# Two stacked transformer blocks on one core: GpSimd's splits in four pieces, query scales moved into the copies out of PSUM, and another order at the start of each layer's projections

## The reference

```
x = layer_norm(alpha * x + 0.5 * swiglu(x, ffn_w_gu[l, 0], ffn_w_down[l, 0]), ln_g[l, 0], ln_b[l, 0])
mix = token_mixers(x, w_in[l], ...)
x = layer_norm(alpha * x + mix, ln_g[l, 1], ln_b[l, 1])
x = layer_norm(alpha * x + 0.5 * swiglu(x, ffn_w_gu[l, 1], ffn_w_down[l, 1]), ln_g[l, 2], ln_b[l, 2])
```

```
s = jnp.einsum('bqhgd,bkhd->bhgqk', qi, k).astype(jnp.float32) * scale
p = jax.nn.softmax(s, axis=-1)
o = jnp.einsum('bhgqk,bkhd->bqhgd', p.astype(v.dtype), v)
```

## Time and profile before

| | us |
|---|---|
| median of 3 runs | 1860.24 |
| lowest, highest | 1855.27, 1863.33 |
| profiled execution | 1861.57 |
| its span | 1859.8 |
| TensorE busy | 1660.4 (89%) |
| VectorE busy | 867.8 (47%) |
| ScalarE busy | 661.6 (36%) |
| GpSimd busy | 242.7 (13%) |
| mean granted TensorE clock | 0.939 |

### The profile page before, as it was taken

The page is one execution under the profiler, slowest core; times in us unless marked ns, Lnnn a source line. Parts: engine busy times, 40 slices in busy tenths (PEclk is TensorE's granted clock), DMA queues, the critical chain, the costliest instruction groups (busy, mean ns, idle before and its releaser), DMA issues.

```text
span 1859.8 us, 29654 instructions
## 1 busy us (share of the span) xinstructions
PE 1660.4 (89%) x11817; PEld 1325.8 (71%) x11817; DVE 867.8 (47%) x1292; ACT 661.6 (36%) x965; POOL 242.7 (13%) x182
## 2 busy tenths in 40 slices
PE   8989997677667776999999999999999999899997
PEld 6777874343223332899977779998999977779996
DVE  4684542011101111555565656555655575665555
ACT  5454441111101111343433544444334333544442
POOL 1223210000000000000133323001300133232000
PEclk9999998887788888999999999999999999899999
DMA  9514476999999999945533055436454542054511
GB/s 387 181 47 142 176 271 262 426 425 426 426 426 426 426 426 402 357 170 186 198 138 134 1 182 204 178 120 247 170 197 175 198 152 103 7 211 179 191 45 45
DMA packets 60951, 421.41 MB, mean 227 GB/s; under 512 B 7008, under 2 KB 16064, under 8 KB 17216
## 3 DMA queue, kind: packets, MB, share of 16 engines
q1 hardware_dynamic: 59136, 409.13, 56.1%
q10 hardware_dynamic: 1728, 11.03, 1.7%
HBM read 419.08 MB, written 1.05 MB: 226 GB/s over the span
## 4 chain that ended last, share of the span: by engine, by line
PE 62%; SPq 13%; DMA 8%; DVE 5%; issue 4%; ACT 3%; POOL 3%; DVEq 0%; ACTq 0%; POOLq 0%
PE bank L964 26%; SPq L1618 13%; PE bank L1005 12%; DMA ring<-in_we 7%; PE bank L1697 6%; PE bank L1739 6%; PE bank L1765 2%; DMA ring<-in_wf 1%; PE bank L1882 1%; PE bank L1900 1%; PE bank L983 1%; POOL small L534 1%; PE bank L604 1%; PE bank L1877 1%; PE bank L990 1%
## 5 line engine op out<-in xcount | busy, mean ns | idle before, releaser
L964 PE MATMUL bank<-xh,wlu 128*128 128x256 f32 x1344 | 379.9, 283 | 0.0
L964 PE MATMUL bank<-xh,whu 128*128 128x256 f32 x1344 | 379.8, 283 | 0.0
L964 PE MATMUL bank<-xl,whu 128*128 128x256 f32 x1344 | 379.8, 283 | 0.0
L964 PEld LDWEIGHTS bank<-xh,whu 128*128 128x128 f32 x1344 | 257.0, 191 | 3.3
L964 PEld LDWEIGHTS bank<-xl,whu 128*128 128x128 f32 x1344 | 257.0, 191 | 3.3
L964 PEld LDWEIGHTS bank<-xh,wlu 128*128 128x128 f32 x1344 | 257.2, 191 | 0.0
L873 DVE TENSOR_TENSOR wlu<-ring,whu 128x2048 fp32r<-128x2048 f32 x84 | 196.1, 2334 | 50.9 <-ACT whu L868 50.9
L873 DVE TENSOR_TENSOR wld<-ring,whd 128x1024 fp32r<-128x1024 f32 x88 | 108.2, 1229 | 189.2 <-ACT whd L868 189.2
L868 ACT ACTIVATE whu<-ring 128x2048 fp32r (+1 forms) x88 | 167.1, 1901 | 3.0 <-DMA ring<-in_wf 3.0
L868 ACT ACTIVATE whd<-ring 128x1024 fp32r (+1 forms) x88 | 93.2, 1060 | 207.1 <-PE bank L1005 203.7
L604 PE MATMUL bank<-ring,xg 128*32 128x256 f32 x1472 | 110.4, 436 | 48.7 <-DMA ring<-in_we 46.3
(11 more groups left out here) (319 smaller groups left out, 2808.3 us busy)
## 6 DMA issues: line engine op xcount, KB each, us to landing
ring<-in_we SPq DMA_DIRECT2D x144, 1024.0 KB, 26.9
ring<-in_wf SPq DMA_DIRECT2D x88, 1536.0 KB, 6.6
ring<-in_w SPq DMA_DIRECT2D x52, 1024.0 KB, 4.8
more<-in_we SPq DMA_DIRECT2D x48, 1024.0 KB, 25.7
ring<-in_w SPq DMA_DIRECT2D x32, 256.0 KB, 3.6
ln<-in_ln ACTq DMA_DIRECT2D x6, 1024.0 KB, 4.8
bias<-in_bias ACTq DMA_DIRECT2D x2, 2048.0 KB, 7.8
bias<-in_bias SPq DMA_DIRECT2D x1, 2048.0 KB, 19.7
```

The source lines that it names most:

```text
L964: ins = pe.matmul(bank[4 + p][:, m * S:(m + 1) * S], w[p][:, cols], v[:, k], start=(k == 0 and n == 0), stop=(k == KD - 1 and n == 2))
```

## The change

- Every split by GpSimd (and its one copy to a high part) is issued as four operations on 512 columns instead of one on 2048. The semaphore goes up after the fourth.
- At the start of a layer's projections GpSimd splits the second chunk too, right behind the first; ScalarE makes its high part without waiting for the end of the feed-forward; VectorE no longer splits it, and makes high part and rest of x pair by pair.
- `pe_part` runs the first chunk in two rounds: all products with the high part of x, for which it waits for that part alone, then those with the rest.
- Axial and latent units have scale 1. Their queries are multiplied by 64 ** -0.5 and 96 ** -0.5 in the copy out of PSUM, which becomes a tensor_scalar; the scale of the maximum goes.

```diff
@@ -382,12 +382,12 @@
             q, _ = head_rows(qkT2, 8 + at_q // 2, 64 * (at_q % 2), 64)
             _, k = head_rows(qkT2, 7, 64 * kv, 64)
             c = C0 + 384 + 64 * kv
-            units2.append(Unit([q], [k], [proj2[:, t, c:c + 64] for t in range(NT)], 64 ** -0.5,
+            units2.append(Unit([q], [k], [proj2[:, t, c:c + 64] for t in range(NT)], 1.0,
...
-            units2.append(Unit([q], [k], [vm[:, t, h, :] for t in range(NT)], BQ ** -0.5,
+            units2.append(Unit([q], [k], [vm[:, t, h, :] for t in range(NT)], 1.0,
...
@@ -483,12 +487,16 @@
-        def low(eng, run, c):
+        def low(eng, run, c, step=None):
 
             eng.wait_ge(dh_ok, run.high + (c + 1))
             n, s = run.width(c), run.slots[c]
-            eng.tensor_tensor(slot_r[s][:, 0:n], slot[s][:, 0:n], run.highs[c % 2][:, 0:n].bitcast(F32),
-                              ALU.subtract).then_inc(dlp_ok if c < 2 else dlv_ok, 1)
+            step = step or n
+            for c0 in range(0, n, step):
+                part = slice(c0, c0 + step)
+                ins = eng.tensor_tensor(slot_r[s][:, part], slot[s][:, part], run.highs[c % 2][:, part].bitcast(F32),
+                                        ALU.subtract)
+            ins.then_inc(dlp_ok if c < 2 else dlv_ok, 1)
...
@@ -873,6 +881,13 @@
+        def ffn_low_pieces(eng, t, p, done):
+
+            for c0 in range(0, 2 * D, 512):
+                ins = eng.tensor_tensor(wlu[p][:, c0:c0 + 512], ring[:, ring_tile(t) + c0:ring_tile(t) + c0 + 512],
+                                        whu[p][:, c0:c0 + 512].bitcast(F32), ALU.subtract)
+            ins.then_inc(done, 1)
...
@@ -1171,17 +1186,15 @@
-            if then is None:
+            if paired:
+                for q in range(4):
+                    top(q)
+                    rest(q)
+            else:
                 for q in range(4):
                     top(q)
                 for q in range(4):
                     rest(q)
-            else:
-                for q in range(4):
-                    top(q)
-                    rest(q)
-                    if q == 0:
-                        then()
...
@@ -1307,7 +1320,6 @@
                 run = run2(l, 0)
-                act.wait_ge(f_dn, (l * 2 + 1) * (FT + 1))
                 act_high(act, run, 1)
                 act_norm(act, st, l * 3)
...
@@ -1359,11 +1371,7 @@
-                def second():
-                    dve.wait_ge(dlp_ok, run.low_p + 1)
-                    low(dve, run, 1)
-
-                dve_norm_T(dve, l * 3, xTh2, (0, 1), second)
+                dve_norm_T(dve, l * 3, xTh2, True)
...
@@ -1419,9 +1427,10 @@
-                def group(n, b, inc=1):
+                def group(n, b, inc=1, scale=1.0):
                     dve.wait_ge(t_ps, tb + (n + 5 if n < 3 else n + 7))
-                    dve.tensor_copy(qkT2[:, 2 * n:2 * n + 2].rearrange("p k s -> p (k s)"), bank[b][:]).then_inc(t_out, inc)
+                    dve.tensor_scalar(qkT2[:, 2 * n:2 * n + 2].rearrange("p k s -> p (k s)"), bank[b][:], scale, None,
+                                      ALU.mult).then_inc(t_out, inc)
...
@@ -1453,13 +1462,14 @@
                     if u == 7:
-                        group(4, 6)
+                        group(4, 6, scale=64 ** -0.5)
                     if 9 <= u < 13:
                         j = u - 9
                         dve.wait_ge(t_ps, tb + (12 + j))
                         at_b = 10 + 4 * (j % 2) + 2 * (j // 2)
-                        dve.tensor_copy(qkT2[0:BQ, at_b:at_b + 2, :],
-                                        bank[7 - j % 2][0:BQ].rearrange("p (b s) -> p b s", b=2)).then_inc(t_out, 1)
+                        dve.tensor_scalar(qkT2[0:BQ, at_b:at_b + 2, :],
+                                          bank[7 - j % 2][0:BQ].rearrange("p (b s) -> p b s", b=2),
+                                          (BQ ** -0.5, 1.0)[j % 2], None, ALU.mult).then_inc(t_out, 1)
@@ -1513,7 +1523,8 @@
-                low(pool, run2(l, 0), 0)
+                for c in range(2):
+                    low(pool, run2(l, 0), c, 512)
                 for i in range(NT):
                     pool.wait_ge(var_ok, l * VAR2 + (VAR1 + 1 + i))
                     inverse_root(pool, rs[:, i:i + 1])
@@ -1552,9 +1563,11 @@
                 pool.sem_inc(hi_go, 1)
-                pool.tensor_copy(run.highs[0], slot[run.slots[0]]).then_inc(dh_ok, 1)
+                for c0 in range(0, CH, 512):
+                    ins = pool.tensor_copy(run.highs[0][:, c0:c0 + 512], slot[run.slots[0]][:, c0:c0 + 512])
+                ins.then_inc(dh_ok, 1)
                 for c in range(2):
-                    low(pool, run, c)
+                    low(pool, run, c, 512)
@@ -1679,7 +1692,10 @@
             for c in range(first, end):
-                if tb is not None:
+                split = tops is not None and c == first
+                if split:
+                    pe.wait_ge(xh_ok, tops)
+                elif tb is not None:
                     pe.wait_ge(t_out, tb + (c - first + 1))
...
@@ -1699,7 +1716,14 @@
-                if c < end - 1:
+                if split:
+                    for passes in ((0, 1), (2,)):
+                        if passes == (2,):
+                            pe.wait_ge(t_out, tb + 1)
+                        for kk in range(per):
+                            for i in range(NT):
+                                ins = products(kk, i, halves, passes)
+                elif c < end - 1:
...
@@ -1965,8 +1989,7 @@
             if unit.bias is None:
-                st.link(dve.tensor_reduce(nmax[:, b], src, X, ALU.max, negate=True))
-                dve.tensor_scalar(nmax[:, b], nmax[:, b], unit.scale, None, ALU.mult).then_inc(lg_ok, 1)
+                dve.tensor_reduce(nmax[:, b], src, X, ALU.max, negate=True).then_inc(lg_ok, 1)
                 return
...
@@ -2054,27 +2077,27 @@
-            low1(pool, 1)
+            low1(pool, 1, 512)
...
```

More of the change, by code:

```diff
@@ L458, in high1_of, with low1 @@
             act.activation(high1[n % 2], slot[n % SLOTS1], ACT.Copy).then_inc(dh_ok, 1)
-        def low1(eng, n):
+        def low1(eng, n, step=None):
             eng.wait_ge(dh_ok, n + 1)
-            eng.tensor_tensor(slot_r[n % SLOTS1], slot[n % SLOTS1], high1[n % 2].bitcast(F32),
-                              ALU.subtract).then_inc(low_at(n)[0], 1)
+            step = step or CH
+            for c0 in range(0, CH, step):
+                part = slice(c0, c0 + step)
+                ins = eng.tensor_tensor(slot_r[n % SLOTS1][:, part], slot[n % SLOTS1][:, part],
+                                        high1[n % 2][:, part].bitcast(F32), ALU.subtract)
+            ins.then_inc(low_at(n)[0], 1)
         def run2(l, r):
@@ L898, in pool_second @@
             pool.wait_ge(wh_ok, g * FFN_W + 2)
-            ffn_low(pool, 1, 1, False, pre_ok)
+            ffn_low_pieces(pool, 1, 1, pre_ok)
         def pool_affine(pool, st, j, after):
@@ L1078, in dve_ffn @@
             else:
-                dve_norm_T(dve, l * 3 + (f - 1 if f == 0 else 1), xh, range(4))
+                dve_norm_T(dve, l * 3 + (f - 1 if f == 0 else 1), xh)
             dve.wait_ge(wh_ok, g * FFN_W + 3)
@@ L1159, in act_norm_T, with dve_norm_T @@
                     ins.then_inc(xf_ok, 1)
-        def dve_norm_T(dve, j, high, first, then=None):
+        def dve_norm_T(dve, j, high, paired=False):
             def pair(t, q):
@@ L1212, in pe_layers @@
                         pe.wait_ge(den_v, l * 3 + (DENV1 + 1))
-                    pe_part(pe, run2(l, 0), n, xTh2, xl, n, tb if n == 0 else None)
+                    pe_part(pe, run2(l, 0), n, xTh2, xl, n, *((tb, None, l * 12 + 5) if n == 0 else ()))
                 pe.wait_ge(den_a, l * 3 + (DENA1 + 2))
@@ L1672, in pe_tiles_T, with pe_part @@
                         ins.then_inc(t_ps, 1)
-        def pe_part(pe, run, part, xh, xl, n, tb=None, banks=None):
+        def pe_part(pe, run, part, xh, xl, n, tb=None, banks=None, tops=None):
             sel = 4 * (n % 2)
@@ L1690, in pe_part, with products @@
                           for w in (run.highs[c % 2], slot_r[run.slots[c]]))
-                def products(kk, i, columns):
+                def products(kk, i, columns, passes=range(3)):
                     k = (c - first) * per + kk
-                    for m, (v, w) in enumerate(((xh, wh), (xh, wl), (xl, wh))):
+                    for m in passes:
+                        v, w = ((xh, wh), (xh, wl), (xl, wh))[m]
                         for c0 in columns:
@@ L2060, in _ @@
             heads(1, 2 * AH, AD)
-            low1(pool, 12)
-            low1(pool, 13)
+            low1(pool, 12, 512)
+            low1(pool, 13, 512)
             for h in range(RH):
@@ L2065, in _ @@
                 power(pool, st, rs, mean[:, :, 1], 1.0, GN_EPS)
-            low1(pool, 14)
+            low1(pool, 14, 512)
             key_roots(0)
             key_roots(1)
-            low1(pool, 18)
-            low1(pool, 19)
```

(8 more changed lines are left out.)

## The result

| | median us | runs | ratio to before, 95% interval |
|---|---|---|---|
| before | 1860.16 | 1855.27 to 1863.33 (6) | 1 |
| after | 1848.38 | 1846.70 to 1850.69 (6) | 0.9934 [0.9917, 0.9950] |

The change saves 11.8 us, 0.66%. The forecast was 1848. The profiled execution of after took 1846.70 us with a span of 1844.9; that of before 1861.57 with 1859.8. So the traces differ by 14.9 us.

The account below looks back on a forecast made before the run. TensorE bounds the kernel (62% of the chain), so only its idle time or low clock pays. Profiled 1861.57 us: +0.15 - 0.4 - 12.8 + 0.45 = -12.6, 1849.0; against the median 1848, 8-in-10 range 1842 to 1859.

Parts of the forecast that it names:

- block 1, three waits for splits: TensorE's waits for GpSimd splits at 19.21, 170.75 and 196.06 us each grow by 0.45: +1.35 us.
- block 1, held operations: VectorE operations held by GpSimd at 91.17 and 129.28 us are freed earlier: -0.65 and -0.55 us.
- entry, per layer: Start of each layer's projections: transposes 0.55 us later, first product 0.75 gained by needing only the rounded part; net -0.2 us.
- border of the layers: TensorE waits for the norm's inverse root, which follows GpSimd's quartered split directly: +0.45 us.
- The mixer's stall and clock: Last mixer units: 1.66 us gap goes (-1.9) and TensorE's clock stays up (-4.5): -6.4 us per layer, 12.8 for both.
- rival 1: TensorE's clock falls in the mixer's tail all the same: 1853 us, or 1857 if at once in both layers; chance 0.28.
- late in both: Case of rival 1: the clock falls late in both layers' mixer tails, about 4.5 us less gain, 1853 us.
- tax: Extra time of a GpSimd split issued as four pieces: +0.45 us per split, bounds nothing and 0.55.
- -0.65 for L2422: Block 1: L2422 is free after one quarter, but later VectorE operations meet quarters, so only ScalarE is earlier; bounds 0, -3.1.
- The product at 129.28: Block 1: product L2472 starts 3.3 us earlier, but only TensorE's 0.61 us of idle time goes: -0.55 us.
- Rival 2: The mixer's wait moves to another late operation; gap over 1 us and slow clock stay: about 1858 us; chance 0.15.
- Rival 3: VectorE operations of every kind are stopped at each GpSimd quarter, in mixer and entry: slower, about 1868 us; chance 0.05.

Follow-up runs that it names:

- e3_fillers: Kernel before with six filler products of zeros on TensorE in the mixer's 1.66 us gap, scaling and stall kept: 1852.70 us, ratio 0.9947.
- e4_whole: Changed kernel with GpSimd's splits and copy whole again instead of in quarters: 1845.02 us, ratio 0.9912 to the kernel before.
- e1_scales: Kernel before with only the mixer's small scaling removed and its factor moved into the copies out of PSUM: 1850.57 us, ratio 0.9933.
- e2_quarters: Kernel before with only GpSimd's splits and copy cut into quarters, scaling and entry kept: 1849.88 us, ratio 0.9926.
- e6_entry: Changed kernel with the old entry of the projections back, quarters and scales as changed: 1849.63 us, ratio 0.9927 to the kernel before.
- e7_two: Changed kernel with whole splits and copy except block 1's splits at 91 and 127 us, left in quarters: 1847.32 us, ratio 0.9917 to before.
- e7_again: Same kernel as e7_two, timed again beside the later filler kernels: 1846.96 us, ratio 0.9912 to the kernel before.
- e9_gap: Kernel of e7_two plus nine zero fillers in TensorE's 2.27 us idle time before the projections' last big chunk: 1844.16 us, ratio 0.9893 to before.
- e10_gap_tail: Kernel of e9_gap plus three zero fillers before the values of each of the last two mixer units: 1846.62 us, ratio 0.9898 to before.

## Why the prediction was right

The forecast's sum was -12.6 us from execution to execution; the traces give -14.9. Step by step, by TensorE's starts in the two traces:

| term | predicted | measured |
|---|---|---|
| block 1, three waits for splits | +1.35 | +0.43 +0.33 +0.41 = +1.2 |
| block 1, other idle steps between 135 and 246 us | 0 | +0.4 (stretch 111.64 to 112.80, less two of these waits) |
| block 1, held operations | -1.2 | -2.1 (transposes at 75 to those at 135 us: 59.85 to 57.79) |
| start of the program, no part of the change | 0 | -0.6 (first product 11.32 to 10.76) |
| entry, per layer | -0.2 | +0.41 -0.72 = -0.3 (idle 0.85 to 1.26, 1.70 to 0.98) |
| border of the layers | +0.45 | +0.5 (transposes to transposes 196.89 to 197.41) |
| mixer's tail, layer 0 (unit at 1053.53 to the product at 1076.06) | -6.4 | -6.9 (22.53 to 15.66) |
| mixer's tail, layer 1 | -6.4 | -4.1 (22.46 to 18.34) |
| clock near 989 in layer 0 and behind the border | not counted | some -2 and -1.2 |
| all other stretches | 0 | +0.5 |

**The mixer's stall and clock** were seen in the right place, and the clock was priced rightly for the case that it stays up: it is worth 4.7 in layer 1 of e3_fillers, against the 4.5 taken, and what remains of layer 0's 6.9 is 2.1 for the stall, against 1.9. But that case is the rarer one in the traces. In after's layer 1 rival 1 came true in part: the clock fell late in the tail, which gives back 2.7 (124.76 us from product to product in after's layer 1, 122.08 in e4_whole, where the tail kept its clock). The same stretch (from the unit at 1053.53 in before to the first product behind the mixer, us) in every traced kernel without the gap and without fillers in it:

| kernel | layer 0 | layer 1 |
|---|---|---|
| before, with the gap | 22.53 | 22.46 |
| after | 15.66 | 18.34 |
| e1_scales | 18.29 | 18.41 |
| e2_quarters | 18.77 | 18.71 |
| e4_whole | 15.66 | 15.67 |
| e6_entry | 18.28 | 18.42 |
| e7_two | 18.43 | 18.44 |
| e7_again | 18.30 | 18.33 |
| e9_gap | 18.43 | 17.15 |

Where it took 15.7 the clock stayed up; in the thirteen others of the sixteen it fell at the last idle steps. So the gap brought the fall early and for 13.7 us; without the gap it mostly still comes, for some 7. A tail with the late fall is 4.1 shorter than before and not 6.4, and that is rival 1's "late in both": two late falls cost 5.4, against the 4.5 that it took. With 18.4 in both layers the change's terms (block 1 -0.5, entry -0.6, border +0.5) add up to -8.8, with 15.7 in both to -14.3. The medians' 11.8 lies between. How often each case comes isn't known: five of these eight traces are of executions slower than their kernel's median. That the sum met the median so closely is partly luck.

**What was wrong in it** is the credit. The prediction gave the mixer's gain to the scaling that goes, and saw in the quarters only a tax and block 1. e1_scales and e2_quarters show that either takes the whole gap away. The prediction's sentence "a held VectorE operation waits at most 1.3 us instead of up to 4.5" held the answer; it wasn't carried to L1969, where 2.81 would have become 1.2: 1.6 us less for a gap of 1.66.

**Block 1** came out 0.9 better in its held operations. The term that was mis-sized most is the -0.65 for L2422, which measured -1.3: VectorE did arrive only 0.4 us earlier (96.00 for 96.58, with 0.14 from before), but TensorE's idle step of 1.17 us at 101.28 went altogether, since ScalarE, freed first, fed it. The unit behind it came 1.4 us earlier (107.41 for 108.83). The product at 129.28 gave 0.8 instead of 0.55. The bounds given for block 1, +1.4 and -2.5, don't follow from its terms: with the stated bounds of the tax they would be +1.65 and -3.65. The measured -0.5 lies inside both.

**Entry and border** were right within 0.1 us: GpSimd's inverse root stands at 939.47, directly behind the split (934.51 + 5.00). The 2.3 us taken off VectorE show in no start of TensorE's, as said.

**Rival 2** fell: no operation took the place of the scaling. **Rival 3** fell: the maximum took 0.69 us and the reciprocal 0.17 while GpSimd's pieces ran (1051.25 to 1056.20). The Trainium skill's page "SBUF — State Buffer" (Who interferes with whom) says that tensor_reduce never contends with GpSimd; the 0.69 us agree. It also says that the holder keeps the port for its whole instruction, which is borne out by the operations at 91.02 to 94.75, each let go when one piece of about 1.24 us ends.

**Open:** why a given idle step lets the clock fall in one run or layer and not in another. The same 2.27 us of idle time stand before 987.46 and 1531.69 in after, and the clock fell behind the second alone. The fastest of after's runs was the one profiled, and the falls that it lacked (near 989, in layer 0's tail, behind the border) look like luck of that run: 14.9 us between traces, 11.8 between medians. Only one run of after and one of before has a trace, so this is argued and not shown. The Trainium skill's page "TensorE: Matmul & The Clock Gate" (Part 1: The HAM clock gate) says that the moment at which the clock rises varies from run to run. The traces show a varying moment for the fall: in after's layer 1 it came 0.1 us before the product behind the last idle step of 0.78 us, in e1_scales' layer 0 0.9 us behind that product's start. They also show falls near 989, 1063 and 1607 us present in some executions and absent in others.

## What to carry to other kernels

When VectorE is held by a GpSimd instruction, look first for the one small operation that is late, and remove it or cut the long instruction that holds it: here either gave as much as the whole change, as far as the times can tell. Cut only those splits beside which somebody is late; every cut costs 0.4 us where a reader waits for the split itself. Price an idle step of TensorE together with what the clock does behind it (4.7 us of clock for 1.66 us of idle time in layer 1), and ask whether the fall would come a little later without that step: here it mostly did, and 2.7 of it came back. Don't expect every step filled with zeros to pay: the fall may come elsewhere.

## What was not expected of the hardware

A fall of the clock costs very different amounts by where it comes. In the mixer between 1027 and 1049 us it lasted 17 us with TensorE busy for 17.00 of them; in the dense products near 989 it was over within 4 us. And filling idle time changed where it fell more than how often. Between 760 and 1830 us the clock of e10_gap_tail, which stayed up near 983 and 1538 us and over both tails, was low for some 20 us in the profiled run (17 from 1027, 3.4 from 1297), that of the changed kernel for some 10 (3.4 from 1531, 6.8 from 1607), and that of e4_whole, with no fillers added, for 3.4 (from 1532).
